# Attention units of a two-part transformer kernel: outputs made by feature, probabilities rescaled before they are turned, gates turned by VectorE

## The chip, the cores and the metric

One core of a Trainium2 chip runs the whole program. The metric is the device time of one execution in microseconds (us), as a median over runs. The core's engines are TensorE (PE; its weight loads are shown apart as PEld), VectorE (DVE), ScalarE (ACT), GpSimd (POOL) and SyncE (SP); each takes its instructions strictly in the order of the program, and they wait for each other on semaphores.

## The reference, cut to what matters

256 tokens of 2048 features go through a first block (state-space and gated-linear-attention mixer, then a feed-forward part) and then twice through this layer:

```python
def _layer(x, ...):                     # DEPTH_2 = 2 layers, all in float32
    h = _rms_norm(x, g_pre)
    proj = h @ w_in                     # a_q a_k a_v a_g | b_cq b_ckv b_kr b_g | c_q c_k c_v c_g
    ...
    o_a = attention(qa, ka, va)  * silu(a_g)      # 8 heads, 2 key/value heads, head size 128
    ...
    o_b = attention(q_full, k_full, vb) * silu(b_g)   # 4 heads, queries and keys of 128 + 64
    o_c = neighbourhood_attention(qc, kc, vc, rpb) * silu(c_g)   # 4 heads, bias and mask
    y = concat([o_a, o_b, o_c]) @ w_out
    return x + _rms_norm(y, g_post)
```

with attention = softmax(q k^T * scale) v for each head. The change touches what stands after the softmax's exponential: the division by the sum, the product with v, the gate, and the layout in which w_out's product reads the result.

## The kernel before

**The stream.** Nearly all of the time is one stream of matrix products. The weights are cut into pieces of 256 rows by 512 columns (`places`, piece number p). SP fetches a piece into a ring of four (`raw`), ACT rounds it to fp32r (`w_hi`, L1015), DVE takes the rest (`w_lo`, L1673), and PE makes twelve 128x512 products with it, the lines L983, L984 and L985 in turn (x_hi by w_lo, x_hi by w_hi, x_lo by w_hi; two k-tiles, two token tiles t). `w_hi` and `w_lo` are rings of eight. At step p, ACT and DVE convert piece p + 4 (AHEAD), then drain the block of pieces that has just ended (`result`), and then do side work that has come due (`beside.reach(p)`). PE does piece p and then its own side work of step p. So on every engine the order of the work is fixed: conversion, drain, side work.

**Drains.** Sums of block b stand in banks 2*(b%2) and 2*(b%2)+1. ACT takes the first token tile, DVE the second (L2357 or L2358, drain_dve), at piece `drain_at` of the next block, which is 3, or 1 where that block has only two pieces. PE waits for the drain of block b-2 before it begins block b. POOL then stores the block to DRAM, by one DMA (L2494), or, for the blocks in `by_feature`, by eight DMAs from `turned_store` (L231), which lay it out so that a later load brings it by feature, up to a transpose inside squares of 32 by 32.

**Attention units.** Each layer has four units of four heads: a0 and a1 (key "a", `grouped`), b (`latent_unit`) and c (`neighbour`). A unit starts at its own piece number; its scores come 10 pieces later, and I call the step of the scores s. From there ATTEND sets the steps: exponentials at s+1, first turn of the probabilities (turn0, L848) at s+3, product with the values for token tile 0 (values0, L858) and the turn for tile 1 at s+5, values1 at s+7, and the output turned by PE (L665) at s+9.

In a unit PE writes scores (L831, and L839 in b) to banks 4 to 7. DVE takes the row maxima (L2228; in c it first adds the bias, L2224, so that the maxima take longer), ACT makes the exponentials and their sums (L1453), PE turns the probabilities into banks 4 and 5, ACT copies them to `pt` (L1459), and PE multiplies them by the values into bank 6 or 7 with tokens on the partitions. The gate has come from DRAM by token, ACT makes its silu (L1473), DVE scales it by one over the sums (L2239, L2245) and multiplies it by the output (L2249). PE turns the product (`gated`, L665), ACT rounds it to x_hi (L1025) and DVE takes x_lo (L1684).

In c the bias is loaded by POOL (`biases`, L2500 and L2504) once unit b is over and the stores ahead of it are issued; DVE adds the mask to it (L2318) at s-1.

Of the kernel before, what the change touches and what calls it, by code (L numbers as in the profile page):

```python
# [96 lines left out]
ATTEND = {"exp": 1, "turn0": 3, "values0": 5, "values1": 7, "out": 9}  # L97
# [302 lines left out]
def emit(nc, ctx, values, i, out):  # L400
# [60 lines left out]
    by_feature.update({("proj2", col): None for col in (C2_Q, C2_K)})  # L461
# [155 lines left out]
    class Grouped:  # L617
        def __init__(self):
            room = Room(work2)
            self.q, self.k, self.v, self.gate = room(NT, UW), room(NT, HD), room(NT, HD), room(NT, UW)  # L620
            self.qt, self.kt, self.pt = room(UNIT_H, S), room(1, S), room(UNIT_H, S)
            self.tmp, self.tmp2 = room(NT, UW), room(NT, UW)
# [13 lines left out]
    class LatentUnit:  # L636
        def __init__(self):
# [7 lines left out]
            self.gate = room(NT, UW)  # L645
            self.probs = [four(self.q), four(self.qt)]

    class Neighbour:
        def __init__(self):
            room = Room(work2)  # L650
            self.q, self.k, self.v, self.gate = room(C_H, S), room(C_H, S), room(NT, UW), room(NT, UW)
            self.qt, self.kt, self.pt = room(C_H, S), room(C_H, S), room(UNIT_H, S)
            self.bias, self.mask = room(NT, C_H * S), room(NT, S)
# [6 lines left out]
    def tensor():  # L660
# [164 lines left out]
        def attend(key, at, q_of, k_of, value, probs, pt, gate, rotated=None):  # L825
# [17 lines left out]
            def turn_probs(t):  # L843
                pe.wait_ge(*unit.act["exp", *key, t, 3])
# [7 lines left out]
            def times_values(t):  # L852
# [12 lines left out]
            pe.wait_ge(*unit.act["exp", *key, 1, 3])  # L865
# [5 lines left out]
            yield at + ATTEND["out"]  # L871
            for t in range(NT):
                pe.wait_ge(*unit.dve["gated", *key, t])
                turn(6 + t, gate[:, t, :]).then_inc(*unit.pe("turned_out", *key, t))

        def grouped(l, u):
# [7 lines left out]
                              lambda h, kt: ga.v[:, kt, :], ga.probs, ga.pt, ga.gate)  # L884

        def latent_unit(l):
# [10 lines left out]
                              lambda h, kt: lu.kv[:, kt, h * 2 * HD + HD:(h + 1) * 2 * HD], lu.probs, lu.pt, lu.gate,  # L897
                              (lu.qpe, lu.kpe))

        def neighbour(l):  # L900
            key = (l, "c", 0)
            yield from attend(key, UNIT_STEP["scores"], lambda h: nu.qt[:, h, :], lambda h: nu.kt[:, h, :],
                              lambda h, kt: nu.v[:, kt, h * HD:(h + 1) * HD], nu.probs, nu.pt, nu.gate)
# [102 lines left out]
    def scalar():  # L1006
# [438 lines left out]
        def attend(key, at, probs, pt, scale, of_bias, gate, gate_col, x0):  # L1445
# [26 lines left out]
            for t in range(NT):  # L1472
                A(gate[:, t, :], gate[:, t, :], ACT.Silu).then_inc(*unit.act("gate", *key, t))  # L1473
            yield at + ATTEND["out"]
            for t in range(NT):
                act.wait_ge(*unit.pe["turned_out", *key, t])
                high(6 + t, x0, t).then_inc(*unit.act("out_hi", *key, t))

        def fetch_gate(key, gate, col):
            all_stored(start_of["dram", "proj2", col // BLK * BLK if col < C2_CQ else col, key[0]])  # L1480
            act.dma_start(gate, proj2[:, :, col:col + UW]).then_inc(*gate_in(*key))

        def grouped(l, u):
            key = (l, "a", u)
            if u:
                act.wait_ge(*unit.pe["turned_out", l, "a", u - 1, NT - 1])
# [25 lines left out]
        def latent_unit(l):  # L1512
            key = (l, "b", 0)
            act.wait_ge(*unit.pe["turned_out", l, "a", 1, NT - 1])
# [16 lines left out]
        def neighbour(l):  # L1531
            key = (l, "c", 0)
            act.wait_ge(*unit.pe["turned_out", l, "b", 0, NT - 1])
# [132 lines left out]
    def vector():  # L1666
# [547 lines left out]
        def attend(key, at, probs, scale, bias, gate, x0):  # L2214
# [22 lines left out]
            def one_over_sums(t):  # L2237
                dve.wait_ge(*unit.act["exp", *key, t, 3])
                dve.reciprocal(small[:, 2 + t, 0:4], small[:, 2 + t, 0:4]).then_inc(*unit.dve("recips", *key, t))  # L2239

            def gates(t):
                dve.wait_ge(*unit.act["gate", *key, t])
# [388 lines left out]
```

## Time and profile before

| what | value |
|---|---|
| median of 3 runs | 2846.88 us (2844.66 to 2848.42) |
| span of the profiled execution | 2842.5 us |
| PE busy | 2818.7 us, 99% |
| PEld busy | 2335.3 us, 82% |
| DVE busy | 1841.9 us, 65% |
| ACT busy | 1445.1 us, 51% |
| POOL busy | 198.4 us, 7% |

The profile is of one execution; its span runs from the first to the last recorded instruction and stands 4.4 us below the median of the runs. No other time of that execution is given. A matmul's record overlaps that of the next, so a stretch of PE is read by the starts of its instructions and not by their lengths.

### The profile page before, as it was taken

The page shows a single profiled execution, that of the slowest core. Times are in us where ns is not written, and L with a number is a line of the kernel's source. Part 1 is how long each engine was busy: PE and PEld are TensorE (multiplying, and loading weights), DVE is VectorE, ACT ScalarE, POOL GpSimd, SP SyncE. Part 2 cuts the span into 40 slices and gives each one's busy share as a digit, 9 for nine tenths or more (in the row PEclk, how much of TensorE's full clock was granted, in tenths as well). Part 3 has the DMA queues.
Part 4 walks back from the last instruction along what each step waited for, and adds up shares of the span by engine and source line. Part 5 has one row for each costly group of instructions (what it writes and reads, how often), then busy time and mean ns, then how long its engine had stood idle before and what let it go on. Part 6 is the DMA issues. An engine that isn't in the chain of part 4 may idle for free. (4 is left out here: it accounts for less than half of the span.)

```text
span 2842.5 us, 34753 instructions
## 1 busy us (share of the span) xinstructions
PE 2818.7 (99%) x13414; PEld 2335.3 (82%) x13414; DVE 1841.9 (65%) x2311; ACT 1445.1 (51%) x1959; POOL 198.4 (7%) x309
## 2 busy tenths in 40 slices
PE   9999999999999999999999999999999999999998
PEld 8888888888888878888888888888888888888887
DVE  6477787777755757567656556565666556676556
ACT  5455565556554655444444434344545445645544
POOL 1200000000000000000102001020000020000110
PEclk9999999999999999999999999999999999999999
DMA  7778888888877778775767676676576667776675
GB/s 254 244 254 277 267 290 284 278 281 282 257 230 236 249 230 293 240 254 165 255 212 222 207 207 208 207 229 200 170 266 204 216 213 225 221 230 220 219 219 184
DMA packets 386148, 667.71 MB, mean 235 GB/s; under 512 B 65709, under 2 KB 95261, under 8 KB 384958
## 3 DMA queue, kind: packets, MB, share of 16 engines
q1 hardware_dynamic: 271104, 510.33, 56.0%
q10 hardware_dynamic: 97614, 104.65, 11.7%
q0 software_dynamic: 17264, 50.50, 5.5%
q8 instruction: 106, 1.74, 0.2%
q14 instruction: 60, 0.49, 0.1%
HBM read 609.34 MB, written 56.03 MB: 234 GB/s over the span
## 5 line engine op out<-in xcount | busy, mean ns | idle before, releaser
L1673 DVE TENSOR_TENSOR w_lo<-raw,w_hi 128x1024 fp32r<-128x1024 f32 (+2 forms) x976 | 1156.5, 1205 | 710.1 <-ACT w_hi L1015 702.7
L983 PE MATMUL bank<-w_lo,x_hi 128*128 128x512 f32 (+2 forms) x3888 | 1524.6, 392 | 8.5 <-DVE w_lo L1673 4.7
L985 PE MATMUL bank<-w_hi,x_lo 128*128 128x512 f32 (+2 forms) x3888 | 1508.0, 388 | 0.0
L984 PE MATMUL bank<-w_hi,x_hi 128*128 128x512 f32 (+2 forms) x3888 | 1507.2, 388 | 0.0
L1015 ACT ACTIVATE w_hi<-raw 128x1024 fp32r<-128x1024 f32 (+2 forms) x976 | 995.3, 1044 | 861.7 <-PE bank L985 370.3
L983 PEld LDWEIGHTS bank<-w_lo,x_hi 128*128 128x128 f32 x3888 | 730.8, 188 | 163.0 <-issue 9.6
L985 PEld LDWEIGHTS bank<-w_hi,x_lo 128*128 128x128 f32 x3888 | 730.4, 188 | 150.4
L984 PEld LDWEIGHTS bank<-w_hi,x_hi 128*128 128x128 f32 x3888 | 731.0, 188 | 147.3 <-issue 2.9
L1025 ACT ACTIVATE x_hi<-bank 128x512 fp32r<-128x512 f32 (+1 forms) x96 | 53.5, 587 | 159.2 <-PE bank L665 144.9
L231 POOL DMA_DIRECT2D hidden<-arena x96 | 61.7, 650 | 895.1 <-DVE arena L2415 894.3
L2494 POOL DMA_DIRECT2D proj<-stage x48 | 34.4, 717 | 1193.1 <-DVE stage L2358 688.0
L1684 DVE TENSOR_TENSOR x_lo<-bank,x_hi 128x512 fp32r<-128x512 f32 (+1 forms) x96 | 61.5, 671 | 76.9 <-ACT x_hi L1025 76.9
L231 POOL DMA_DIRECT2D proj<-stage x96 | 61.8, 652 | 264.6 <-DVE stage L2358 171.9
L1034 ACT ACTIVATE arena<-arena 128x2 f32<-128x2 f32 (+2 forms) x38 | 7.8, 204 | 81.2 <-DVE arena L1693 80.9
L1459 ACT ACTIVATE arena<-bank 128x512 f32<-128x512 f32 x32 | 17.3, 594 | 54.5 <-PE bank L848 54.5
L665 PEld LDWEIGHTS bank<-ident,arena 128*128 128x128 f32 x280 | 32.6, 140 | 13.9 <-issue 3.2
L2245 DVE TENSOR_TENSOR arena<-arena 128x512 f32<-128x512 f32 x16 | 11.0, 689 | 50.5 <-ACT arena L1473 50.5
L665 PE MATMUL bank<-ident,arena 128*128 128x128 f32 x280 | 39.2, 274 | 4.5 <-DVE arena L2054 1.7
L1123 ACT ACTIVATE arena<-arena 128x128 f32<-128x128 f32 x128 | 39.0, 388 | 0.0
L1687 DVE STREAM_TRANSPOSE bank<-arena 128x512 f32<-128x512 f32 x48 | 32.6, 709 | 6.9 <-DMA arena<-hidden 4.8
L1453 ACT ACTIVATE arena<-bank,arena 128x256 f32<-128x256 f32 x48 | 24.9, 540 | 20.7 <-DVE arena L2232 12.6
L2358 DVE COPY stage<-bank 128x512 f32<-128x512 f32 (+1 forms) x48 | 32.3, 673 | 0.3 <-ACT stage L1586 0.2
(225 smaller groups left out, 1318.3 us busy)
## 6 DMA issues: line engine op xcount, KB each, us to landing
raw<-in_w_in SPq DMA_DIRECT2D x492, 512.0 KB, 5.0
raw<-in_w_up SPq DMA_DIRECT2D x128, 512.0 KB, 4.2
raw<-in_w_down SPq DMA_DIRECT2D x128, 512.0 KB, 4.5
raw<-in_w_out SPq DMA_DIRECT2D x96, 512.0 KB, 4.8
arena<-proj ACTq DMA_DIRECT2D x74, 512.0 KB, 5.3
raw<-in_w_ssd_branch SPq DMA_DIRECT2D x64, 512.0 KB, 5.4
proj<-stage POOLq DMA_DIRECT2D x48, 512.0 KB, 5.6
raw<-in_w_gla_branch SPq DMA_DIRECT2D x32, 512.0 KB, 4.9
```

The source lines that it names most:

```text
L231: dma(to[:, :, b, :].rearrange("m p f -> p m f"), tile[part, t, :].rearrange("p (m f) -> p m f", f=SQUARE)).then_inc(*signal())
L665: op = pe.transpose(bank[b][:, k * P:(k + 1) * P], source[:, k * P:(k + 1) * P], ident[:, :])
L983: pe.matmul(o, x_hi[:, xk, tokens(t)], w_lo[:, r, k, 0:b.n], start=a, stop=False)
L984: pe.matmul(o, x_hi[:, xk, tokens(t)], w_hi[:, r, k, 0:b.n], start=False, stop=False)
L985: op = pe.matmul(o, x_lo[:, xk, tokens(t)], w_hi[:, r, k, 0:b.n], start=False, stop=z_)
L1015: A(w_hi[:, p % SPLIT_RING, 0:b.per, 0:b.n], raw[:, p % RAW_RING, 0:b.per, 0:b.n], ACT.Copy).then_inc(*split_hi(p))
L1025: return A(x_hi[:, x0:x0 + n, tokens(t)], full, ACT.Copy)
L1123: op = A(dec[:, t, h, :], dec[:, t, h, :], ACT.Relu, bias=gt[:, CS + t, h:h + 1], scale=-1.0)
L1673: TT(w_lo[:, p % SPLIT_RING, 0:b.per, 0:b.n], raw[:, p % RAW_RING, 0:b.per, 0:b.n], w_hi[:, p % SPLIT_RING, 0:b.per, 0:b.n].bitcast(F32), ...
L1684: return TT(x_lo[:, x0:x0 + n, tokens(t)], full, x_hi[:, x0:x0 + n, tokens(t)].bitcast(F32), ALU.subtract)
L1687: return dve.transpose(to, source)
L2494: pool.dma_start(to, drained[:, b.half, :, 0:b.n]).then_inc(*stored[b.half](b.number))
```

## The change

Outputs now come by feature. In units b and c the values stand (they are the loaded weights) and the turned probabilities move, four heads by two key tiles, 128 columns each. In a0 and a1, where four heads share one key/value head, one product per key tile moves all four heads, 512 columns. The output needs no turn, so PE's L665 of these units is gone, and so are its wait for `gated` and ACT's wait for it. One over the sum belongs to a token, and tokens now lie along the free axis of the output, so it can't be applied to the gate: DVE multiplies the probabilities by it before PE turns them (`even`, 128x1024 for each token tile), at s+2 and s+4, and PE's turn waits for `even` where it waited for ACT's exponentials. The gate has to come by feature too: the blocks of its columns are stored by `turned_store`, the load is `turned_rows`, and DVE undoes the squares of 32 (`turn`, 128x1024) at s+6, after one silu of 128x1024 on ACT where there were two of 128x512. ACT and DVE take x_hi and x_lo from the gated product in SBUF.

```diff
-ATTEND = {"exp": 1, "turn0": 3, "values0": 5, "values1": 7, "out": 9}
+ATTEND = {"exp": 1, "even0": 2, "turn0": 3, "even1": 4, "values0": 5, "gates": 6, "values1": 7, "out": 9}
...
-    by_feature.update({("proj2", col): None for col in (C2_Q, C2_K)})
+    by_feature.update({("proj2", col): None for col in (C2_Q, C2_K, C2_AG, C2_AG + UW, C2_BG, C2_G)})
...
             def turn_probs(t):
-                pe.wait_ge(*unit.act["exp", *key, t, 3])
+                pe.wait_ge(*unit.dve["even", *key, t])
...
                 pe.wait_ge(*unit.act["pt", *key, t])
-                for hh in range(UNIT_H):
+                if key[1] == "a":
                     for kt in range(NT):
-                        op = pe.matmul(bank[6 + t][:, hh * HD:(hh + 1) * HD], pt[:, hh, kt * P:(kt + 1) * P],
-                                       value(hh, kt), start=(kt == 0), stop=(kt == NT - 1))
+                        op = pe.matmul(by_tile(bank[6 + t]), value(0, kt), pt[:, :, kt * P:(kt + 1) * P],
+                                       start=(kt == 0), stop=(kt == NT - 1))
+                for hh in range(0 if key[1] == "a" else UNIT_H):
+                    for kt in range(NT):
+                        op = pe.matmul(bank[6 + t][:, hh * P:(hh + 1) * P], value(hh, kt), pt[:, hh, kt * P:(kt + 1) * P],
+                                       start=(kt == 0), stop=(kt == NT - 1))
...
-            pe.wait_ge(*unit.act["exp", *key, 1, 3])
             times_values(0)
...
-            yield at + ATTEND["out"]
-            for t in range(NT):
-                pe.wait_ge(*unit.dve["gated", *key, t])
-                turn(6 + t, gate[:, t, :]).then_inc(*unit.pe("turned_out", *key, t))
...
-            for t in range(NT):
-                A(gate[:, t, :], gate[:, t, :], ACT.Silu).then_inc(*unit.act("gate", *key, t))
+            A(flat(gate), flat(gate), ACT.Silu).then_inc(*unit.act("gate", *key))
...
-                act.wait_ge(*unit.pe["turned_out", *key, t])
-                high(6 + t, x0, t).then_inc(*unit.act("out_hi", *key, t))
+                act.wait_ge(*unit.dve["gated", *key, t])
+                A(x_hi[:, x0:x0 + UNIT_H, tokens(t)], gate[:, :, tokens(t)], ACT.Copy).then_inc(
+                    *unit.act("out_hi", *key, t))
...
-            act.dma_start(gate, proj2[:, :, col:col + UW]).then_inc(*gate_in(*key))
+            act.dma_start(gate, turned_rows(by_feature["proj2", col])).then_inc(*gate_in(*key))
...
-            def one_over_sums(t):
+            def even(t):
                 dve.wait_ge(*unit.act["exp", *key, t, 3])
                 dve.reciprocal(small[:, 2 + t, 0:4], small[:, 2 + t, 0:4]).then_inc(*unit.dve("recips", *key, t))
-
-            def gates(t):
...
                 dve.wait_ge(*unit.dve.now)
+                TT(probs[t], probs[t], wide(small[:, 2 + t, 0:4].unsqueeze(2), [P, UNIT_H, S]), ALU.mult).then_inc(
+                    *unit.dve("even", *key, t))
+
+            def gated(t):
                 dve.wait_ge(*unit.pe["values", *key, t])
-                TT(gate[:, t, :], gate[:, t, :], bank[6 + t][:, :], ALU.mult).then_inc(*unit.dve("gated", *key, t))
+                TT(gate[:, :, tokens(t)], by_tile(bank[6 + t]), gt[:, :, tokens(t)], ALU.mult).then_inc(
+                    *unit.dve("gated", *key, t))
...
-            yield at + ATTEND["turn0"]
-            one_over_sums(0)
-            one_over_sums(1)
-            yield at + ATTEND["values0"]
-            gates(0)
+            yield at + ATTEND["even0"]
+            even(0)
+            yield at + ATTEND["even1"]
+            even(1)
+            yield at + ATTEND["gates"]
+            dve.wait_ge(*unit.act["gate", *key])
+            turn(flat(gt), flat(gate)).then_inc(*unit.dve("gt", *key))
+            dve.wait_ge(*unit.dve.now)
+            gated(0)
             yield at + ATTEND["values1"]
-            gates(1)
+            gated(1)
```

**Where rows stand now.** On VectorE, unit c of the first layer, from the last maxima (L2232 before, L2233 now) to the drain of a w_out block (L2435, now L2439). Before:

```order
L2232 TENSOR_SCALAR arena<-arena 128x4 [waits unit_dve]
L1673 TENSOR_TENSOR w_lo<-raw,w_hi 128x1024 [waits split_hi] x3
L2435 COPY arena<-bank 128x512 [waits summed]
L2435 COPY arena<-bank 128x512
L2239 RECIPROCAL arena<-arena 128x4 [waits unit_act] x2
```

and now:

```order
L2233 TENSOR_SCALAR arena<-arena 128x4 [waits unit_dve]
L1674 TENSOR_TENSOR w_lo<-raw,w_hi 128x1024 [waits split_hi] x2
L2240 RECIPROCAL arena<-arena 128x4 [waits unit_act]
L2242 TENSOR_TENSOR arena<-arena 128x1024 [waits unit_dve]
L1674 TENSOR_TENSOR w_lo<-raw,w_hi 128x1024 [waits split_hi]
L2439 COPY arena<-bank 128x512 [waits summed]
```

The reciprocal and the rescaling (L2242) stand behind the conversions of steps s+1 and s+2, and ahead of the one of s+3.

On VectorE, unit a0 of the first layer, from the conversions after the maxima to the gate; L2357 (now L2361) drains the block of queries for a1. Before:

```order
L1673 TENSOR_TENSOR w_lo<-raw,w_hi 128x1024 [waits split_hi] x3
L2357 TENSOR_SCALAR stage<-bank,arena 128x512 [waits drain_act,edge_act,stored0,summed]
L2239 RECIPROCAL arena<-arena 128x4 [waits unit_act] x2
L1673 TENSOR_TENSOR w_lo<-raw,w_hi 128x1024 [waits split_hi] x2
L2245 TENSOR_TENSOR arena<-arena 128x512 [waits unit_dve,unit_act]
L2249 TENSOR_TENSOR arena<-arena,bank 128x512 [waits unit_pe,unit_dve]
```

and now:

```order
L1674 TENSOR_TENSOR w_lo<-raw,w_hi 128x1024 [waits split_hi] x2
L2240 RECIPROCAL arena<-arena 128x4 [waits unit_act]
L2242 TENSOR_TENSOR arena<-arena 128x1024 [waits unit_dve]
L1674 TENSOR_TENSOR w_lo<-raw,w_hi 128x1024 [waits split_hi]
L2361 TENSOR_SCALAR stage<-bank,arena 128x512 [waits drain_act,edge_act,stored0,summed]
L1674 TENSOR_TENSOR w_lo<-raw,w_hi 128x1024 [waits split_hi]
L2240 RECIPROCAL arena<-arena 128x4 [waits unit_act]
L2242 TENSOR_TENSOR arena<-arena 128x1024 [waits unit_dve]
L1674 TENSOR_TENSOR w_lo<-raw,w_hi 128x1024 [waits split_hi] x2
L1688 STREAM_TRANSPOSE arena<-arena 128x1024 [waits unit_act]
L2247 TENSOR_TENSOR arena<-bank,arena 128x4x128 [waits unit_pe,unit_dve]
```

The first rescaling has come in ahead of the drain.

On TensorE, the first turn of the same unit a0 (step s+3), with bank numbers; the row after the turn begins the block of gates for a1. Before:

```order
L985 MATMUL bank3<-w_hi,x_lo 128x512
L848 MATMUL bank4<-ident,arena 128x128 [waits unit_act]
L848 MATMUL bank4<-ident,arena 128x128 x3
L848 MATMUL bank5<-ident,arena 128x128 x4
L983 MATMUL bank0<-w_lo,x_hi 128x512 [waits split_lo,drain_dve]
```

and now:

```order
L986 MATMUL bank3<-w_hi,x_lo 128x512
L850 MATMUL bank4<-ident,arena 128x128 [waits unit_dve]
L850 MATMUL bank4<-ident,arena 128x128 x3
L850 MATMUL bank5<-ident,arena 128x128 x4
L984 MATMUL bank0<-w_lo,x_hi 128x512 [waits split_lo,drain_dve]
```

The order of this place is as it was; the turn waits for VectorE instead of ScalarE, and the product behind it waits for the drain that has moved back on VectorE.

## Rows read from the trace of the kernel before

**Rows 1.** The page: busy us, share of the span, instructions of each engine.
```profile
PE 2818.7 (99%) x13414; PEld 2335.3 (82%) x13414; DVE 1841.9 (65%) x2311; ACT 1445.1 (51%) x1959; POOL 198.4 (7%) x309
```

**Rows 2.** Waits of PE, first layer's units: total us, times, longest.
```profile
PE bank L821 <- DVE arena L2194: 0.8, 1, 0.8
```

**Rows 3.** Chain that ended last, longest pieces: start, us, what.
```profile
2560.44 3.45 PE bank L831 x16
...
2586.56 1.78 PE bank L858 x16
2593.83 0.87 PE bank L665 x8
```

**Rows 4.** Timeline of PE, a0's output turned: start, us, engine, line.
```profile
2182.45 0.40 PE L985 MATMUL bank<-w_hi,x_lo 128*128 128x512 f32 x1
2182.69 1.04 PE L665 MATMUL bank<-ident,arena 128*128 128x128 f32 x8
...
2183.80 0.40 PE L984 MATMUL bank<-w_hi,x_hi 128*128 128x512 f32 x1
```

**Rows 5.** Timeline, first layer's unit c, all engines.
```profile
2372.97 2.00 ACT L1015 ACTIVATE w_hi<-raw 128x1024 fp32r<-128x1024 f32 x2
2373.18 1.04 PE L848 MATMUL bank<-ident,arena 128*128 128x128 f32 x8
2374.05 2.36 DVE L1673 TENSOR_TENSOR w_lo<-raw,w_hi 128x1024 fp32r<-128x1024 f32 x2 [1.98 <-ACT w_hi L1015]
```

**Rows 6.** Sources of lines: ns min/median/max, first and last start.
```profile
L2318 DVE TENSOR_TENSOR arena<-arena x4: 1219/1222/1222, 2360.8 to 2771.6; 128x1024 f32<-128x1024 f32 x4
L2239 DVE RECIPROCAL arena<-arena x16: 148/160/174, 2161.2 to 2788.6; 128x4 f32<-128x4 f32 x16
```

**Rows 7.** Timeline, first layer's unit a0, all engines.
```profile
2158.22 2.36 DVE L1673 TENSOR_TENSOR w_lo<-raw,w_hi 128x1024 fp32r<-128x1024 f32 x2 [2.64 <-ACT w_hi L1015]
2160.50 0.74 DVE L2357 TENSOR_SCALAR stage<-bank,arena 128x512 f32<-128x512 f32 x1
2160.73 1.02 PEld L848 LDWEIGHTS bank<-ident,arena 128*128 128x128 f32 x8
...
2161.75 0.48 PE L983 MATMUL bank<-w_lo,x_hi 128*128 128x512 f32 x1
2164.10 2.36 DVE L1673 TENSOR_TENSOR w_lo<-raw,w_hi 128x1024 fp32r<-128x1024 f32 x2 [2.70 <-ACT w_hi L1015]
...
2169.07 1.04 PE L848 MATMUL bank<-ident,arena 128*128 128x128 f32 x8
```

**Rows 8.** Busy time by stretch: PE, PEld, DVE, ACT, POOL, granted clock, DMA share, GB/s.
```profile
38.00:41.00 3.00, 3.00 (x9) 2.33 (x8) 2.45 (x2) 1.33 (x2) 1.07 (x2) 0.50 0.90 283
2553.00:2556.00 3.00, 2.52 (x16) 2.11 (x17) 2.93 (x9) 1.39 (x4) 0.00 (x0) 1.00 0.58 180
```

**Rows 9.** Timeline of PE, at the start and at second layer's a0.
```profile
36.63 0.47 PE L983 MATMUL bank<-w_lo,x_hi 128*128 128x512 f32 x1 [1.94 <-DVE w_lo L1673]
...
37.85 0.57 PE L985 MATMUL bank<-w_hi,x_lo 128*128 128x512 f32 x1
...
41.50 0.39 PE L985 MATMUL bank<-w_hi,x_lo 128*128 128x512 f32 x1
...
2553.48 1.50 PE L821 MATMUL bank<-ident,arena 128*128 128x128 f32 x10 [0.59 <-DVE arena L2194]
```

**Rows 10.** Timeline of POOL and DVE up to c's bias; landing of L2504.
```profile
2282.17 5.13 POOL L231 DMA_DIRECT2D proj<-stage  x8 [19.76 <-DVE stage L2357]
2333.83 0.72 POOL L2494 DMA_DIRECT2D proj<-stage  x1 [22.86 <-DVE stage L2357]
...
2335.25 9.87 POOL L2504 DMA_DIRECT2D arena<-skew  x16
DMA to landing us min/median/max: 7.0/7.5/8.4
2360.76 2.35 DVE L2318 TENSOR_TENSOR arena<-arena 128x1024 f32<-128x1024 f32 x2
```

More of the change, by code:

```diff
@@ L644, in __init__ @@
             self.tmp = room(B_H, B_ROPE)
-            self.gate = room(NT, UW)
+            self.gate, self.gt = room(UNIT_H, S), self.kt
             self.probs = [four(self.q), four(self.qt)]
@@ L823, in turn_heads, with attend @@
             op.then_inc(*unit.pe(*key))
-        def attend(key, at, q_of, k_of, value, probs, pt, gate, rotated=None):
+        def attend(key, at, q_of, k_of, value, probs, pt, rotated=None):
             yield at
@@ L883, in grouped @@
             yield from attend(key, UNIT_STEP["scores"], lambda h: ga.qt[:, h, :], lambda h: ga.kt[:, 0, :],
-                              lambda h, kt: ga.v[:, kt, :], ga.probs, ga.pt, ga.gate)
+                              lambda h, kt: ga.v[:, kt, :], ga.probs, ga.pt)
         def latent_unit(l):
@@ L1485, in grouped @@
             if u:
-                act.wait_ge(*unit.pe["turned_out", l, "a", u - 1, NT - 1])
+                act.wait_ge(*unit.pe["values", l, "a", u - 1, NT - 1])
                 act.wait_ge(*unit.dve["out_lo", l, "a", u - 1, NT - 1])
@@ L1513, in latent_unit @@
             key = (l, "b", 0)
-            act.wait_ge(*unit.pe["turned_out", l, "a", 1, NT - 1])
+            act.wait_ge(*unit.pe["values", l, "a", 1, NT - 1])
             act.wait_ge(*unit.dve["out_lo", l, "a", 1, NT - 1])
@@ L1532, in neighbour @@
             key = (l, "c", 0)
-            act.wait_ge(*unit.pe["turned_out", l, "b", 0, NT - 1])
+            act.wait_ge(*unit.pe["values", l, "b", 0, NT - 1])
             act.wait_ge(*unit.dve["out_lo", l, "b", 0, NT - 1])
@@ L2212, in with_gain, with attend @@
             op.then_inc(*unit.dve("sin", l, name))
-        def attend(key, at, probs, scale, bias, gate, x0):
+        def attend(key, at, probs, scale, bias, gate, gt, x0):
             yield at
@@ L2262, in attend @@
                 dve.wait_ge(*unit.act["out_hi", *key, t])
-                lower(6 + t, x0, t).then_inc(*unit.dve("out_lo", *key, t))
+                TT(x_lo[:, x0:x0 + UNIT_H, tokens(t)], gate[:, :, tokens(t)],
+                   x_hi[:, x0:x0 + UNIT_H, tokens(t)].bitcast(F32), ALU.subtract).then_inc(*unit.dve("out_lo", *key, t))
         def grouped(l, u):
@@ L2288, in grouped @@
             dve.wait_ge(*unit.act["root", *key, "q"])
-            yield from attend(key, UNIT_STEP["scores"], ga.probs, None, None, ga.gate, KT + 4 * u)
+            yield from attend(key, UNIT_STEP["scores"], ga.probs, None, None, ga.gate, ga.gt, KT + 4 * u)
         def latent_unit(l):
@@ L2305, in latent_unit @@
                      lambda a: wide(a, [P, 2, B_ROPE]))
-            yield from attend(key, UNIT_STEP["scores"], lu.probs, QW ** -0.5, None, lu.gate, KT + A_H)
+            yield from attend(key, UNIT_STEP["scores"], lu.probs, QW ** -0.5, None, lu.gate, lu.gt, KT + A_H)
         def neighbour(l):
@@ L2321, in neighbour @@
             yield from attend(key, UNIT_STEP["scores"], nu.probs, HD ** -0.5,
-                              nu.bias.rearrange("p t (h n) -> p t h n", h=C_H), nu.gate, KT + A_H + B_H)
+                              nu.bias.rearrange("p t (h n) -> p t h n", h=C_H), nu.gate, nu.gt, KT + A_H + B_H)
         def times_gain(l, j, ts=tuple(range(NT))):
@@ L2496, in biases @@
         def biases(l):
-            pool.wait_ge(*unit.pe["turned_out", l, "b", 0, NT - 1])
+            pool.wait_ge(*unit.pe["values", l, "b", 0, NT - 1])
             pool.wait_ge(*unit.dve["out_lo", l, "b", 0, NT - 1])
@@ L2508, in residual @@
         def residual(l):
-            pool.wait_ge(*unit.pe["turned_out", l, "c", 0, NT - 1])
+            pool.wait_ge(*unit.pe["values", l, "c", 0, NT - 1])
             pool.wait_ge(*unit.dve["out_lo", l, "c", 0, NT - 1])
```

15 lines of the change are left out of this document (6 added, 9 removed).

## The prediction

> **What bounds the kernel now.** I read the page first: PE is busy 99% of the span, and nothing else comes near it [rows 1]. Then I read PE's waits in the stretch of the first layer's four units: one, of 0.8 us, before a turn of rotated queries that this change leaves alone [rows 2]. So time saved here is saved on PE's own instructions, and any wait that PE gets is paid in full. The chain that ended last lists the pieces of PE's work in a unit: sixteen 256-column instructions of the scores take 3.45 us, the sixteen of a values product 1.78 us (eight float32 products, two instructions each), and the eight turns of an output 0.87 us [rows 3]. Last I read the timeline around the points where the new waits stand; there the reader is to look at when VectorE starts a conversion, and when PE starts its turn [rows 5, 7].
>
> **What PE loses of its work.** The output turn goes, eight times (four units, two layers). In the timeline, the L985 ahead of it starts at 2182.45 and the L984 behind it at 2183.80 [rows 4]: 1.35 us for what without the turn would be two steps of 0.227 us (twelve products of 128x512 take 2.72 us in the undisturbed stream; nine of them in 2.04). That is 0.89 us each, 7.1 us in all, against 0.87 us by the chain. Values of a0 and a1: before, sixteen instructions of 128 columns in 1.78 us; now four of 512. A 256-column instruction of the scores costs 3.45/16 = 0.216 us [rows 3], so four of 512 cost 4 x 0.431 = 1.72 us. Eight such products save 0.06 us each, 0.5 us. From above it is bounded by two single-pass 512-column steps for each instruction, 4 x 0.454 = 1.82 us, or 0.3 us lost; I take 0.5 saved. In b and c the count and the shape of the products stay. Sum: 7.6 us saved.
>
> **What VectorE gets.** Reciprocals (0.16 us each) stay. Each unit loses two 128x512 scalings of the gate and gets two 128x1024 scalings of the probabilities and one 128x1024 transpose. For the new scaling the nearest row is L2318, also 128x1024 from SBUF to SBUF with a broadcast operand: 1.22 us [rows 6]; below, it can't be less than a 128x512 one, 0.69 us, nor much more than 1.3. So `even` takes 0.16 + 0.03 + 1.22 = 1.41 us, and it moves what stands behind it by about 1.35 us, since one instruction's end overlaps the next one's start. The work as such is hidden: VectorE is busy 65% [rows 1], and its conversions run up to seven pieces ahead of PE, which needs 2.72 us for each. What is not hidden is where `even` stands.
>
> **Unit c: a new wait of 3.6 us.** The first turn now needs `even(0)`, which stands on VectorE behind the conversion of step s+2. That one waits for ACT's w_hi of the same piece, and ACT makes it only when all eight exponentials are done. In the trace ACT starts it at 2372.97, VectorE starts its conversion at 2374.05, and PE's turn began at 2373.18, before either was ready [rows 5]. Of the pair in the row the second conversion starts 1.14 us after the first (2.36 less 1.22), at 2375.19. In its place now stands `even(0)`, which ends at 2376.60; with 0.05 us for the signal, PE's turn starts near 2376.7 to 2376.8 where it was at 2373.18. That is 3.6 us, twice (the second layer repeats the pattern): 7.2 us. Bounds: 3.0 with a scaling of 0.69 us, 3.9 if the restart costs more. Behind the turn on PE stand all the products of the stream; nothing can pass it.
>
> **Unit a0: a drain comes late.** PE's turn is at 2160.96, its first weight load at 2160.73. VectorE's conversion starts at 2158.22, so `even(0)` ends at 2158.22 + 1.14 + 1.41 = 2160.77 [rows 7]: just too late for the load by 0.1 us. The block that PE begins right after the turn waits for L2357, which ended at 2161.24, half a microsecond before PE began at 2161.75 [rows 7]. `even(0)` now stands ahead of it and pushes it back by 1.35 us, to 2162.6; PE starts the block at 2162.65 instead of 2161.75. That is 0.9 us, twice: 1.8 us (0.4 to 1.1 each). In a1 the same 0.1 us for the turn, and no drain behind it that PE needs soon: 0.2 us for both layers. In b the exponentials are shorter and `even(0)` is done when PE comes: nothing. The second turn, at s+5, is covered: in a0 the conversion starts at 2164.10, so `even(1)` ends at 2166.65, and the turn is at 2169.07 [rows 7]; in c the turn itself moves back with PE.
>
> **The clock.** Near the start PE stands idle for 1.94 us, restarts at 36.63, and from about 37.9 to 41.2 the granted clock is 0.50, 1.2 instead of 2.4 GHz [rows 8, 9]. Nine steps, from 37.85 to 41.50, take 3.65 us instead of 2.04: 1.6 us lost. The wait in c is nearly twice as long as that idle stretch. So I add 1.6 us for each c, 3.2 us (0 to 2.5 each). The page TensorE: Matmul & The Clock Gate of the Trainium skill (section "HAM oscillation — how this bites in real kernels") also has the clock fall back to half in waits between bursts; the row at 36.63 agrees.
>
> **POOL and the DMAs.** Four blocks in each layer are stored by eight DMAs (5.13 us of POOL) instead of one (0.72) [rows 10]: 4.4 us more of POOL each. Between such stores POOL idles far longer than that (19.76 us before the one at 2282.17), so only what follows the last store moves: the bias of c. Its sixteen DMAs end at 2345.1, land 7.5 us later, near 2352.6, and would now land near 2357.0; DVE uses the bias at 2360.76 [rows 10]. Covered by 3.7 us; were that cover gone, VectorE would be late in c and PE's wait there would grow by the same amount. The loads of the gates stay one DMA each and are issued four steps, or 11 us, before their use. All this: nothing.
>
> **The sum.** -7.6 (PE's work) + 7.2 (c) + 1.8 (a0) + 0.2 (a1) + 3.2 (clock) = +4.8 us. Made on the profiled execution, whose span is 2842.5 us; the median of the runs is 2846.9, and I add the difference to that: 2851.7 us, 0.17% slower, which a measurement can't tell from no change (it can tell about 0.2%, 5.7 us).
>
> **The rivals.** (B) The waits come, but the clock stays up: +1.6 us, 2848.5. For it: only one drop is in the whole trace. Against it: that one followed a shorter idle stretch. (C) The clock falls in a0 too: turns and two short waits, of 0.1 and 0.9 us, make 1.9 us without a large product. Each drop costs 1.6 us: +8.0, 2854.9, slower. Against it: the second layer's a0 has a wait of 0.59 us and ten turns in one stretch, and the clock there is 1.00 [rows 8, 9]. The skill's page has a rule for it (same title, Part 4, "PE-mode transpose"): transposes don't count as busy for the gate. By that rule this stretch is idle throughout; the trace of those ten turns speaks against a drop at this length. (D) The wait in c doesn't come, because VectorE has `even(0)` ready: then -7.6 + 1.8 + 0.2 = -5.6 us, 2841.3, on the verge of faster. It needs ACT's w_hi of that piece 3.6 us earlier, ahead of the exponentials; below 2 us of waits in all, c included, the change gains more than 0.2%. The fixed order of ACT speaks against it. (E) The bias lands over 3.7 us later than I think (landing in 11 instead of 7.5 us, for POOL's stores now write short rows): from there each microsecond is paid in both layers; with 2 us more, +8.8, and together with other late drains +12, 2858.9.
>
> **How the numbers follow.** My forecast 0.50, B 0.17, C 0.10, D 0.13, E 0.07, and 0.03 for what I don't see. The forecast's own range is 2849 to 2854, by the bounds of the wait in c and of the clock; about three tenths of it lie beyond +5.7 us. Slower: 0.15 from there, C 0.09, E 0.07, rest 0.02, 0.33 in all. Faster: D with something to spare, 0.10, and rest 0.01, so 0.11. Same: 0.56. The range leaves out D and E: 2844.5 to 2857.
>
> **What the profile after would show.** Right: no turns of outputs in the units; PE's longest waits in the layers are two of 3.4 to 3.6 us before the first turn of c, released by L2242, and two near 0.9 us before a large product of a0's next block, released by L2361; a clock of 0.50 for some 3 us behind c's wait. The bias addition L2322 still starts without a wait. Wrong: if no such wait shows, the order of ACT and VectorE was read wrongly, and the time is near 2841; if PE's waits lie at other lines, of w_lo or of the bias, then a cover that I took as ample was not.

## The result, and the profile after

| | before | after |
|---|---|---|
| median of 5 runs each | 2847.9 us | 2857.0 us |
| lowest and highest | 2844.66, 2848.42 | 2855.59, 2862.34 |
| span of the profiled execution | 2842.5 us | 2860.7 us |

The ratio on record is 1.0041, with a 95% interval of 1.0031 to 1.0051: 8.8 to 14.5 us slower, 11.7 by the ratio itself (the two medians of five are 9.1 us apart, inside the interval). "Same" was forecast, +4.8 us; it is a clear loss. The median stands at the upper end of the range (2844.5 to 2857), and 11.7 us on top of the prediction's base of 2846.9 is 2858.6, beyond it. The profiled execution of after was its slowest run, and the span of before's profile is shorter than any of its timed runs, so the two spans are further apart than the medians.

The page of after, against [rows 1]: PE has less work in instructions and more in time, VectorE 18 us more, POOL 35 us more.

```profile
PE 2821.2 (99%) x13254; PEld 2325.3 (81%) x13254; DVE 1860.2 (65%) x2319; ACT 1447.6 (51%) x1951; POOL 233.8 (8%) x365
```

PE's waits in the first layer's units, and then in the second's (total us, times, longest); before, the first layer had one of 0.8 [rows 2]:

```profile
PE bank L850 <- DVE arena L2242: 3.3, 1, 3.3
PE bank L823 <- DVE arena L2195: 2.3, 3, 1.0
PE bank L984 <- DVE stage L2361: 0.9, 2, 0.6
...
PE bank L850 <- DVE arena L2242: 3.3, 1, 3.3
PE bank L823 <- DVE arena L2195: 1.7, 2, 1.1
PE bank L984 <- DVE stage L2361: 1.1, 2, 0.6
```

L850 is the first turn of probabilities, L2242 `even`, L823 a turn of queries or keys that waits for the rotation, L2361 a drain on VectorE. The first two kinds of wait that I forecast are there (c: L850, a0: L2361). The L823 waits are larger than before, which I did not forecast.

Unit c, first layer, timeline of all engines, to be held against [rows 5]:

```profile
2379.84 1.99 ACT L1016 ACTIVATE w_hi<-raw 128x1024 fp32r<-128x1024 f32 x2
2380.92 1.23 DVE L1674 TENSOR_TENSOR w_lo<-raw,w_hi 128x1024 fp32r<-128x1024 f32 x1 [1.97 <-ACT w_hi L1016]
2382.06 0.17 DVE L2240 RECIPROCAL arena<-arena 128x4 f32<-128x4 f32 x1
...
2382.27 1.23 DVE L2242 TENSOR_TENSOR arena<-arena 128x1024 f32<-128x1024 f32 x1
...
2383.55 1.97 PE L850 MATMUL bank<-ident,arena 128*128 128x128 f32 x8 [3.35 <-DVE arena L2242]
...
2386.59 0.63 PE L984 MATMUL bank<-w_lo,x_hi 128*128 128x512 f32 x1
...
2387.87 0.63 PE L984 MATMUL bank<-w_lo,x_hi 128*128 128x512 f32 x1
```

The reader is to see the order on VectorE, conversion, reciprocals, rescaling, and PE's turn right behind it, 2.63 us after the conversion began. I had worked out 2.65 to 2.75. The last two rows are neighbours of the same kind: three products take 1.28 us there instead of 0.68. The granted clock says why (columns as in [rows 8]):

```profile
2380.00:2382.50 2.50, 0.20 (x1) 0.00 (x0) 1.55 (x3) 1.83 (x2) 0.00 (x0) 1.00 1.02 372
...
2383.00:2389.00 6.00, 5.45 (x17) 4.68 (x18) 4.17 (x7) 2.97 (x4) 0.00 (x0) 0.50 0.59 178
...
2390.00:2393.00 3.00, 3.00 (x16) 2.46 (x15) 1.32 (x2) 0.00 (x0) 0.00 (x0) 1.00 0.64 202
```

PE stood idle from 2380.2 to 2383.55, and from 2382.8 on the clock is 1.2 instead of 2.4 GHz for 6.8 us, twice as long as in the drop near the start [rows 8, 9].

Unit a0, against [rows 7]:

```profile
2165.61 1.22 DVE L2242 TENSOR_TENSOR arena<-arena 128x1024 f32<-128x1024 f32 x1
...
2167.01 1.03 PE L850 MATMUL bank<-ident,arena 128*128 128x128 f32 x8
2167.89 0.74 DVE L2361 TENSOR_SCALAR stage<-bank,arena 128x512 f32<-128x512 f32 x1
...
2168.68 0.50 PE L984 MATMUL bank<-w_lo,x_hi 128*128 128x512 f32 x1 [0.64 <-DVE stage L2361]
```

**Where the time went.** All kernels here make the same 3888 triples of stream products in the same order, so their starts can be lined up: the shift of the n-th L984 of after against the n-th L983 of before, and its steps. In the two layers' units: eight steps of -0.89 where the output turn was; -0.15 for the two values products of each a unit; +0.89 and +0.97 at a0's drain; +6.4 and +6.4 at c's first turn; and, not forecast, +1.7 and +0.7 between a0's s+7 and a1's query turn and +1.2 and +1.3 before b's query turn. The rest is below 0.3. They add up to +11.7 us. Another 6 us of shift lie ahead of the layers, in stages that the change leaves alone; two drops of the clock are part of it. The thirteen profiled executions of this and the kernels below have -1.6 to +6.5 there, 3.3 on average: about that much says only that before's one trace was a fast execution, so I leave it out. Single traces scatter inside the layers too. A second profiled execution of the changed kernel (below) has +6.7 there and +6.3 ahead, so that one trace gives the same 11.7 as the ratio is in part luck.

### The profile page after: what moved, and what is told of

Its sections match the earlier page's. It is cut to its first block and busy times, and to the rows that moved or that the text cites. A ratio compares the mean times of both kernels' runs of the same rounds, so it can differ in the third digit from the quotient of the medians.

```text
span 2860.7 us, 34459 instructions
## 1 busy us (share of the span) xinstructions
PE 2821.2 (99%) x13254; PEld 2325.3 (81%) x13254; DVE 1860.2 (65%) x2319; ACT 1447.6 (51%) x1951; POOL 233.8 (8%) x365
## 5 line engine op out<-in xcount | busy, mean ns | idle before, releaser
L984 PE MATMUL bank<-w_lo,x_hi 128*128 128x512 f32 (+2 forms) x3888 | 1528.1, 393 | 12.3 <-DVE w_lo L1674 6.9
L984 PEld LDWEIGHTS bank<-w_lo,x_hi 128*128 128x128 f32 x3888 | 732.1, 188 | 170.6 <-issue 10.2
L231 POOL DMA_DIRECT2D proj<-stage x160 | 103.0, 652 | 404.0 <-DVE stage L2361 219.7
L2498 POOL DMA_DIRECT2D proj<-stage x40 | 28.6, 716 | 1053.2 <-DVE stage L2362 693.0
L1026 ACT ACTIVATE x_hi<-bank 128x512 fp32r<-128x512 f32 (+1 forms) x80 | 44.8, 585 | 116.6 <-PE bank L667 101.0
L1685 DVE TENSOR_TENSOR x_lo<-bank,x_hi 128x512 fp32r<-128x512 f32 (+1 forms) x80 | 51.1, 668 | 55.1 <-ACT x_hi L1026 55.1
L667 PE MATMUL bank<-ident,arena 128*128 128x128 f32 x216 | 30.8, 275 | 6.8 <-DVE arena L2419 2.7
L667 PEld LDWEIGHTS bank<-ident,arena 128*128 128x128 f32 x216 | 25.2, 140 | 14.8 <-issue 4.7
L1443 ACT ACTIVATE arena<-bank 128x512 f32<-128x512 f32 (+1 forms) x24 | 11.5, 545 | 38.6 <-PE bank L823 38.6
```

Of the source, the lines that this page charges most:

```text
L231: dma(to[:, :, b, :].rearrange("m p f -> p m f"), tile[part, t, :].rearrange("p (m f) -> p m f", f=SQUARE)).then_inc(*signal())
L667: op = pe.transpose(bank[b][:, k * P:(k + 1) * P], source[:, k * P:(k + 1) * P], ident[:, :])
L984: pe.matmul(o, x_hi[:, xk, tokens(t)], w_lo[:, r, k, 0:b.n], start=a, stop=False)
L1026: return A(x_hi[:, x0:x0 + n, tokens(t)], full, ACT.Copy)
L1685: return TT(x_lo[:, x0:x0 + n, tokens(t)], full, x_hi[:, x0:x0 + n, tokens(t)].bitcast(F32), ALU.subtract)
```

## The experiments

The theory (T) going in: c's wait, with its clock, and a0's drain come from the place of `even`; the losses around a1 and b come from the gate's transpose, which holds VectorE at s+6 just when conversions are wanted. Rivals: R1, the DMAs with short rows make the loads late; R2, PE gives the time of the missing output turn back at the next query turn, because the loads pace it. Each kernel was timed beside before on the same chip, 5 to 12 runs each, in four batches. One ten-thousandth of ratio is 0.28 us. "Lost around a1 and b" means the steps of the shift between a0's s+7 and a1's query turn and between a1's s+7 and b's query turn, both layers added: 4.9 us in after's trace.

**Rescaling one step earlier.**

```diff
-ATTEND = {"exp": 1, "even0": 2, "turn0": 3, "even1": 4, "values0": 5, "gates": 6, "values1": 7, "out": 9}
+ATTEND = {"exp": 1, "even0": 1, "turn0": 3, "even1": 4, "values0": 5, "gates": 6, "values1": 7, "out": 9}
```

> The changed kernel with one number altered: VectorE rescales the first half of the probabilities one step earlier, behind the conversion of step s+1 instead of s+2. Theory T (in c, PE waits 3.3 us because the rescaling stands behind a late conversion; half as much again is lost to the granted clock of 0.50 that follows; in a0 the rescaling pushes a drain back by 0.9 us): the two waits of c, their clock and the two drain waits of a0 go, 2 x 6.15 + 2 x 0.89 = 14.1 us less than the changed kernel's 2857.0, 2843; the new waits before the turns of queries of a1 and b (1.1 to 1.3 us each, 3.6 us in all) stay. Rival (the exponentials themselves are too late, the place of the rescaling makes no matter): the wait in c stays above 2 us and the time at 2853 or more.

Measured: 0.9997 (0.9988 to 1.0005), 12.5 us below the changed kernel's ratio; 14.1 was expected. PE's waits in the first layer's units:

```profile
PE bank L823 <- DVE arena L2195: 1.2, 2, 0.6
PE bank L984 <- DVE arena L2439: 0.2, 1, 0.2
PE bank L984 <- DVE stage L2361: 0.2, 1, 0.2
```

No L850 is left. Its steps at c are +0.36 twice, since the weight load still waits 0.6 us for `even`; a0's are 0.01. The losses around a1 and b stay, 5.4 us in all (1.4 and 4.0 by layer), as T said.

**Gate turned at s+4, ahead of the silu, too.**

```diff
             even(1)
+            dve.wait_ge(*gate_in[key])
+            turn(flat(gt), flat(gate)).then_inc(*unit.dve("gt", *key))
             yield at + ATTEND["gates"]
             dve.wait_ge(*unit.act["gate", *key])
-            turn(flat(gt), flat(gate)).then_inc(*unit.dve("gt", *key))
...
-            act.wait_ge(*gate_in[key])
-            A(flat(gate), flat(gate), ACT.Silu).then_inc(*unit.act("gate", *key))
+            act.wait_ge(*unit.dve["gt", *key])
+            A(flat(gt), flat(gt), ACT.Silu).then_inc(*unit.act("gate", *key))
```

The rest of the edit hands `gt` to ACT's part of the unit, and `even0` is 1 as in the run above.

> As the run with the earlier rescaling, and the gate's transpose is taken from step s+6 on VectorE to s+4, ahead of ACT's silu, which then works on the turned gate. Theory T (the waits before the query turns of a1 and b come from VectorE: transpose and gating together hold back the conversion at s+6, so the weights behind it are fetched later and the unit's loads stand in a full DMA queue): the conversion at s+6 starts 1.2 us earlier and the waits before the query turns shrink by half or more, 1 to 3 us less than the run with the earlier rescaling alone, near 2841. Rival R1 (the gates' loads and stores in short rows make the DMA slow) and rival R2 (PE, relieved of the output turn, simply reaches the next unit's turn sooner than loads allow): these waits stay, and the time is the same within 1 us.

Measured: 0.9987 (0.9978 to 0.9995), 2.8 us less than the run above, but the two intervals overlap. The losses around a1 and b are 1.5 us, all of it before b in the second layer.

**Gates stored and loaded by token again.**

```diff
-    by_feature.update({("proj2", col): None for col in (C2_Q, C2_K, C2_AG, C2_AG + UW, C2_BG, C2_G)})
+    by_feature.update({("proj2", col): None for col in (C2_Q, C2_K)})
...
-            act.dma_start(gate, turned_rows(by_feature["proj2", col])).then_inc(*gate_in(*key))
+            act.dma_start(flat(gate).rearrange("p (t n) -> p t n", t=NT), proj2[:, :, col:col + UW]).then_inc(*gate_in(*key))
```

> The changed kernel, but the gates' blocks are stored and loaded by token, one DMA each, as before the change; the transpose on VectorE stays, so the units' outputs are gated by values in the wrong places. Rival R1 (short rows slow the DMA, so the loads of a1 and b come late): the waits before the query turns of a1 and b go, up to 3.6 us less than the changed kernel, 2853. Theory T: they stay, 2856 to 2857. Either way the wait of 3.3 us in c stays.

Measured: 1.0040 (1.0027 to 1.0053), as the changed kernel. The interval alone would still let R1's full 3.6 us in (1.0028), but its trace has 5.8 us lost around a1 and b where R1 had nearly none left. R1 falls as the cause of these waits.

**PE kept at work in c's wait.**

```diff
             yield at + ATTEND["turn0"]
+            if key[1] == "c":
+                pe.wait_ge(*unit.dve["max", *key, 1])
+                for _ in range(14):
+                    pe.matmul(bank[7][:, :], x_hi[:, KT, 0:P], flat(x_hi[:, KT:KT + 2, :]), start=True, stop=True)
             turn_probs(0)
```

> The changed kernel, with 14 products of 128x512 on PE into a bank that nobody reads at that time, put into unit c's wait ahead of its first turn of probabilities, so that PE works where it stood idle. If the granted clock of 0.50 behind the wait comes from the idle stretch: the wait's length is filled or nearly so, the clock stays at 1.00, and the time falls by 2 x 2.6 = 5 us, to about 2852 (fillers that last longer than the wait give some of it back). Rival (the slow clock has another cause, or the late work behind c costs the time): no change, 2857.

Measured: 1.0024 (1.0014 to 1.0034), 4.8 us below the changed kernel; the two intervals just overlap (1.0031 to 1.0034). Ten us around the filled wait in each layer:

```profile
2375.00:2385.00 10.00, 9.83 (x48) 7.93 (x48) 7.87 (x10) 5.05 (x8) 0.00 (x0) 1.00 0.68 218
2787.00:2797.00 10.00, 9.83 (x48) 7.93 (x47) 7.21 (x9) 5.71 (x10) 0.00 (x0) 1.00 0.66 211
```

The steps at c are +3.56 and +3.57 instead of 6.4: the turn starts no sooner, and only the slow stretch behind it is gone. The slow clock needs the idle stretch: the fourteen profiled executions of this text hold 22 drops (the one at the very end of each, when the products are done, left aside), and each begins inside an idle stretch of PE of 1.9 to 3.8 us or at most 1.3 us behind it.

**Only the gate turned early** (the second edit without the first).

> The changed kernel with the gate's transpose at s+4 instead of s+6, and nothing else. Theory T: the drain wait behind s+7 and the wait before the query turn of a1 go in both layers (2.4 us in the changed kernel's trace), that of b shrinks in one layer or both; the wait of 3.3 us in c and the drain wait in a0 stay. Ratio to before near 1.003, 2 to 4 us below the changed kernel. Rival (the earlier rescaling in c or a0 is needed for it, the two edits act only together): a1's waits stay, ratio 1.004.

Measured: 1.0025 (1.0014 to 1.0037), 4.6 us below the changed kernel, with overlapping intervals. Around a1 and b 3.1 us. T had said that a1's losses go in both layers; in the first they did not: 1.4 us stay there, of which 1.2 is one wait for a drain. In this execution the same idle stretch in c cost +3.55 in the first layer:

```profile
2378.00:2381.00 3.00, 0.65 (x6) 0.65 (x7) 2.97 (x4) 0.64 (x1) 0.00 (x0) 1.00 0.79 265
2381.00:2384.00 3.00, 3.00 (x17) 2.54 (x15) 2.08 (x4) 2.52 (x4) 0.00 (x0) 1.00 0.62 214
2384.00:2387.00 3.00, 3.00 (x16) 2.50 (x16) 2.97 (x4) 0.47 (x1) 0.00 (x0) 1.00 0.50 165
```

The turn (3.3 us waited for) falls into the first row, and the clock stays at 1.00 behind it. In the second layer it fell, and the step was 6.34.

**Both edits, and each unit's loads one step earlier** (UNIT_FIRST 37 for 38, and each number of UNIT_STEP one more).

> Earlier rescaling, earlier gate transpose, and the loads of each unit issued one step (2.7 us) earlier, with the rest of the unit where it was. If the waits that are left (before b's query turn, 1.3 us in the second layer) come from the unit's loads landing late in a full DMA queue: they go, and the time is 1 to 2 us below the run with both edits, ratio near 0.998. Rival (the earlier issue only pushes the weights behind it back by as much, since the DMA is full): the wait moves to a conversion or a turn one step on, no gain.

Measured: 0.9981 (0.9972 to 0.999), the fastest version here, 5.4 us below before. The losses around a1 and b are 0.4 us. Against the run without this edit it is 1.7 us, too little to tell apart.

**Both edits, and the output turn's cost put back.**

```diff
             times_values(1)
+            yield at + ATTEND["out"]
+            for n in range(8):
+                pe.transpose(bank[4 + n // 4][:, n % 4 * P:(n % 4 + 1) * P], ident[:, :], ident[:, :])
```

> Earlier rescaling and earlier gate transpose, with eight turns of 128x128 by PE put back at s+9 of each unit, on the identity, into banks that nobody reads then, where the output turn had been. They cost what their removal saved: 8 x 0.89 = 7.1 us where nothing else waits, ratio 1.0012 (against 0.9987). Rival R2 (what PE saves by the output turn is given back at the next query turn, because the loads pace it): in a0, a1 and b of both layers the wait before the next turn shrinks by as much, and the time rises by no more than 2 x 0.9 (c) to 5 us.

Measured: 1.0007 (0.9997 to 1.0016), 5.7 us above the run with both edits. The steps at the eight places go from -0.89 to -0.01; losses around a1 and b are 0.9 instead of 1.5 us. So most of the turn's time is real time, and R2 holds at most for a small part of it.

**Gate turned twice at s+6** in the changed kernel (the second transpose waits for the first).

> The changed kernel with the gate's transpose done twice in a row at s+6 on VectorE: 1.24 us more ahead of the conversion that stands behind it. Theory T: what PE loses in a1's neighbourhood and before b's query turn grows, by up to 1.2 us at each of the four places, 2 to 5 us in all, ratio 1.005 to 1.006. Rival (VectorE's extra work there is covered and the late loads have another cause): the same waits as in the changed kernel, ratio 1.004.

Measured: 1.0077 (1.0065 to 1.009), 9.7 us above the mean of the changed kernel's two ratios where I expected 2 to 5. VectorE's extra work is 8 x 1.24 = 9.9 us.

**The changed kernel once more.**

> The changed kernel itself once more, for how far its own waits and its clock differ from one profiled execution to the next. Ratio 1.003 to 1.005. In the trace: c's wait 3.3 us in both layers; behind it the granted clock falls in some and not in all (in four profiled executions with that wait it stood at 0.50 for 6.8, 6.8, 0, 3.4, 0, 6.8, 3.4 and 0 us); a0 0.9 us twice; what is lost around a1 and before b's query turn between 4 and 6 us in all. If theory T has only the noise of one execution behind it, this last sum comes out near the 3.1 of the run with the gate turned early.

Measured: 1.0045 (1.0033 to 1.0057). The losses around a1 and b are 2.2 us in this execution and were 4.9 in the first: below what I expected, and below the 3.1 with the gate turned early. One trace does not tell one transpose from none at these places. The clock behind c's wait of 3.3 us:

```profile
2380.00:2383.00 3.00, 0.57 (x5) 0.57 (x6) 2.97 (x4) 0.72 (x1) 0.00 (x0) 1.00 0.84 291
...
2384.00:2387.00 3.00, 3.00 (x8) 2.31 (x7) 2.05 (x5) 2.53 (x4) 0.00 (x0) 0.50 0.57 186
2387.50:2390.00 2.50, 2.50 (x13) 2.07 (x12) 1.83 (x2) 0.00 (x0) 0.00 (x0) 1.00 0.60 202
```

3.4 us at 0.50 here and in the second layer, and steps of 5.14 and 5.05.

**Earlier rescaling in c alone.**

```diff
-            yield at + ATTEND["even0"]
+            yield at + ATTEND["even0"] - (key[1] == "c")
```

> The changed kernel with the earlier rescaling in unit c alone. c's wait and its clock go: 2 x 3.2 us (a rest of 0.36 us stays by the two runs with the earlier rescaling) and 3 us of clock on average, 9.5 us in all, ratio 1.0007; a0's drain waits (0.9 us, twice) and the waits around a1 and b stay. If the earlier rescaling in c costs something elsewhere (the stage behind c, or the second layer's start), the ratio is above 1.002.

Measured: 1.0006 (0.9998 to 1.0015), 11.1 us below the changed kernel run beside it; 9.5 was expected. The other waits stayed; in this execution the one before b's query turn in the second layer was 2.95 us long.

**No transpose of the gate, and two at s+4.** Since single traces scatter, the last pair asks the medians, with doses: none at s+6, and two at s+4 on top of the earlier rescaling.

```diff
-                TT(gate[:, :, tokens(t)], by_tile(bank[6 + t]), gt[:, :, tokens(t)], ALU.mult).then_inc(
+                TT(gate[:, :, tokens(t)], by_tile(bank[6 + t]), gate[:, :, tokens(t)], ALU.mult).then_inc(
...
-            turn(flat(gt), flat(gate)).then_inc(*unit.dve("gt", *key))
-            dve.wait_ge(*unit.dve.now)
```

> The changed kernel without the gate's transpose on VectorE: the outputs are multiplied by the gate as it was loaded and activated, whose values then stand in the wrong places. With the kernel as changed (one transpose at s+6) and the run with two this makes three doses at the same place. Theory T (the work between the conversions at s+6 is not covered): c's two waits, a0's drain waits and c's clock stay, the losses around a1 and b shrink to what the kernel before has, 1 us or less in all, and the ratio falls from 1.0043 to 1.0025 or below. Rival (the losses around a1 and b come from the missing output turn or from chance, and only a double transpose is too much): the losses stay at 2.3 to 4.9 us and the ratio at 1.004.

Measured: 1.0021 (1.0012 to 1.003), 6.3 us below the mean of the changed kernel's two ratios, and outside both of their intervals. The losses around a1 and b are 3.1 us in its trace, not 1.

> Earlier rescaling and the gate's transpose at s+4, as in the run with both, but the transpose done twice there: 1.24 us more of VectorE at that place, 10 us in all. Theory T says that the place matters and not the amount: at s+4 no conversion is waited for, so the second transpose is covered and the ratio stays at 0.9987, within 1 us or two. Rival (any further work of VectorE in the units is paid, wherever it stands): 3 to 8 us more, as two transposes at s+6 cost, ratio 1.000 to 1.0015.

Measured: 0.9986 (0.9976 to 0.9995), as with one. VectorE does 9.9 us more there, and the time shows none of it.

**The doses side by side**, with a view of ACT's waits that separates them where PE's don't (L1477 takes x_hi of an output, L2247 is the gating on VectorE):

| gate's transposes per unit | ratio to before | ACT's wait for L2247, both layers | next unit's loads late | lost around a1 and b |
|---|---|---|---|---|
| none (with late rescaling) | 1.0021 | 4.0 us | 0.5 us | 3.1 us |
| one at s+6 (same; two runs) | 1.0041, 1.0045 | 13.4 | 1.6, 1.7 | 4.9, 2.2 |
| two at s+6 (same) | 1.0077 | 23.6 | 2.7 | 9.9, of which 1.5 clock |
| one at s+4 (same) | 1.0025 | 4.0 | 0.4 | 3.1 |
| one at s+6 (earlier rescaling) | 0.9997 | 13.4 | 1.8 | 5.4 |
| one at s+4 (earlier rescaling) | 0.9987 | 4.0 | 0.3 | 1.5 |
| two at s+4 (earlier rescaling) | 0.9986 | 4.0 | 0.8 | 2.6 |

The row of ACT's waits (total us, times, longest) in the changed kernel:

```profile
ACT x_hi L1477 <- DVE arena L2247: 13.4, 16, 1.7
```

the same with no transpose:

```profile
ACT x_hi L1477 <- DVE arena L2247: 4.0, 8, 1.2
```

with two at s+6:

```profile
ACT x_hi L1477 <- DVE arena L2247: 23.6, 16, 2.0
```

and the timeline of VectorE at s+6 of a0 in the changed kernel:

```profile
2181.56 1.23 DVE L1674 TENSOR_TENSOR w_lo<-raw,w_hi 128x1024 fp32r<-128x1024 f32 x1 [7.71 <-ACT w_hi L1016]
2182.70 1.24 DVE L1688 STREAM_TRANSPOSE arena<-arena 128x1024 f32<-128x1024 f32 x1
2183.98 0.69 DVE L2247 TENSOR_TENSOR arena<-bank,arena 128x512 f32<-128x512 f32 x1
2184.59 1.22 DVE L1674 TENSOR_TENSOR w_lo<-raw,w_hi 128x1024 fp32r<-128x1024 f32 x1
```

VectorE has just waited 7.71 us for ACT and comes out of it with work in hand: conversions, and in their midst the transpose and the gating. The conversion behind them starts 3.0 us after the first. ACT, ahead of VectorE in the program, stands at L1477 for L2247, with its own next conversions and, behind those, the loads of the next unit. In before the two conversions stood back to back:

```profile
2174.74 2.36 DVE L1673 TENSOR_TENSOR w_lo<-raw,w_hi 128x1024 fp32r<-128x1024 f32 x2
```

At s+4 the same 1.24 us fall into a stretch after which VectorE waits for ACT in any case, 5.65 us in the run with both edits:

```profile
2168.48 1.24 DVE L1688 STREAM_TRANSPOSE arena<-arena 128x1024 f32<-128x1024 f32 x1
2169.64 1.18 DVE L1674 TENSOR_TENSOR w_lo<-raw,w_hi 128x1024 fp32r<-128x1024 f32 x1
2176.47 1.23 DVE L1674 TENSOR_TENSOR w_lo<-raw,w_hi 128x1024 fp32r<-128x1024 f32 x1 [5.65 <-ACT w_hi L1016]
```

The table's column of late loads shows one link further. It counts when ACT issues the first load of a1 and of b, measured against the start of PE's same stream product, less what before has (mean of the four places). Here is a1's load in the first layer, before, in the changed kernel, and with two transposes at s+6:

```profile
2186.25 0.37 ACTq L1495 DMA_DIRECT2D arena<-proj  x1
...
2193.43 0.37 ACTq L1496 DMA_DIRECT2D arena<-proj  x1
...
2194.07 0.37 ACTq L1496 DMA_DIRECT2D arena<-proj  x1
```

The product just ahead of it in before starts at 2185.62, 2191.55 and 2190.77 in the three: the load comes 0.6, 1.9 and 3.3 us behind it. So the dose at s+6 shows in the next unit's loads at each of the four places. The weights' conversions are late only at first: in after VectorE's conversion behind the gating is 1.9 us late by the same measure, but the next whole piece comes 2.3 us early, since ACT no longer waits for PE's turn of the output (6.16 us in before).

## Why the prediction was wrong

**What PE loses of its work: right.** -7.6 forecast; the steps give 8 x 0.89 and 8 x 0.075, that is -7.7. The 0.2 us forecast for a1's first turn did not show.

**Unit c: right in mechanism and size.** The wait was released by L2242 and PE came 3.55 us late where the clock did not interfere; forecast 3.6, twice.

**Unit a0: right.** +0.89 and +0.97, each a drain behind `even`; forecast 0.9. With the earlier rescaling both went (0.01 and 0.06 stay).

**The clock: right on average, too small for the profiled execution.** Over six profiled executions with an idle stretch of 3.3 to 3.8 us in c there are twelve such places. Behind three the clock stayed up, behind six it was 0.50 for 3.4 us (1.4 to 1.6 us lost) and behind three for 6.8 us (2.8 to 2.9 lost): 1.5 us on average, against 1.6 forecast. Both places of after's own profile are of the longest kind, so there the term is 5.7 instead of 3.2. The seven executions in which c's wait was gone or filled show no drop there. Moving c's rescaling alone gives wait and clock together: 11.1 us by the ratios, against 10.4 forecast less the 0.7 that stay.

**The step that failed: "The work as such is hidden: VectorE is busy 65%".** I charged VectorE's new work only where `even` stood ahead of something, and charged the transpose of the gate, at s+6, with nothing. By the ratios it costs 4.6 us (moved to s+4), 2.8 (the same, with the earlier rescaling) or 6.3 (left out), and doubled it costs another 9.7. The first two differences lie within overlapping intervals; the last two do not, and they carry the claim. A mean over the span says nothing of s+6. There VectorE comes out of a wait for ACT with a run of work due at once, and what is put into it moves all that stands behind: the next conversion, the gating, and through ACT's wait for the gating the next unit's loads. The pattern was at hand: both conversions in the rows of a0 waited over 2.6 us for ACT [rows 7], and I read that as slack. Slack ahead of a conversion is no slack behind it.

**The sum, put right.** -7.7 (PE) + 7.1 (c) + 3.0 (clock, on average) + 1.9 (a0) + 3 to 6 (gate's transpose at s+6) = +7 to +10, under the measured +11.7 but reaching into its interval of 8.8 to 14.5. Without the last term it would be +4.3, close to the forecast. In the profiled execution itself: -7.7 + 7.1 + 5.7 + 1.9 + 4.9 = +11.9, against 11.7 read off.

**The rivals.** B (clock stays up) holds at 3 places of 12. C (clock falls at a0 too) did not come. D (no wait in c) needs the earlier order that one number gives, and then the loss is gone: 0.9997, where D had 0.9980, with no price for the gate's transpose. E, late drains and a late bias: the bias was not late (L2322 starts at 2367.60 without a wait), and no run speaks for the short rows.

**What stays open.** That the next unit's loads are issued later is shown; how much of PE's waits some 7 to 14 steps later comes from these loads and how much from the weights' transfers is argued from the timeline, not shown. In the traces these places scatter by more than a single transpose makes: the run without one lost 3.1 us there, one of the two with it 2.2. Nor is it settled what of the 6 us ahead of the layers, beyond the average of 3.3, is chance.

## What to carry to other kernels

An engine that is 65% busy can have bursts in which each microsecond is paid (two transposes at s+6: 9.9 us more work, 9.7 us more time). Place new work by what stands behind it in the engine's order, and look for the spot after which the engine waits anyway: the same transpose cost 3 to 6 us at s+6, and a second one nothing that could be measured at s+4. If an idle stretch can't be avoided on TensorE, count what the clock takes behind it, and if the order is a table of numbers, move the new work by one step before judging the change: here 12.5 us hung on one digit, and the change, well placed, is worth 3.7 us (0.9987). The 5.4 us of the fastest kernel (0.9981) include earlier loads, which before was not given.

## What was unexpected of the hardware

The same idle stretch of 3.3 us in the same place of nearly the same program was followed by a granted clock of 0.50 for 6.8 us, 3.4 us or not at all. The page TensorE: Matmul & The Clock Gate of the Trainium skill (section "HAM oscillation — how this bites in real kernels") has waits between bursts bring the clock down; the runs agree, but only in 9 of 12 cases. The turns of probabilities that fall into the slow stretch take 1.97 us instead of 1.09.
